# The left tap of a three-tap convolution, moved from VectorE to a ScalarE copy and a GpSimd add

## The reference, cut to what matters

```
def conv_ffn(h, w_up, conv_w, conv_b, w_down):     # h: 256 tokens x 1024
    u = h @ w_up                                    # 256 x 5632
    up = jnp.pad(u, ((0, 0), (1, 1), (0, 0)))
    u = sum(up[:, i:i + S] * conv_w[i] for i in range(3)) + conv_b
    a, b = jnp.split(u, 2, axis=-1)                 # 2816 features each
    return (gelu(a) * b) @ w_down
```

## Time and profile before

| | us |
|---|---|
| median of 3 runs | 2159.01 |
| lowest and highest of them | 2156.7, 2159.69 |
| the profiled execution, whole time | 2157.69 |
| its span, first to last instruction | 2155.9 |
| TensorE busy in it | 2129.4 (99%) |
| VectorE busy | 1491.9 (69%) |
| ScalarE busy | 989.4 (46%) |
| GpSimd busy | 376.3 (17%) |

### The profile page before, as it was taken

One profiled execution on the slowest core, in us unless ns is written; L12 is line 12 of the kernel. 1 busy time (PEld: TensorE's weight loads), 2 busy tenths in 40 slices (PEclk: granted clock), 3 DMA queues, 4 the chain that ended last, 5 costly groups with the idle time before them and its releaser, 6 DMA issues.

```text
span 2155.9 us, 36935 instructions
## 1 busy us (share of the span) xinstructions
PE 2129.4 (99%) x14280; PEld 1939.2 (90%) x14280; DVE 1491.9 (69%) x2157; ACT 989.4 (46%) x1462; POOL 376.3 (17%) x262
## 2 busy tenths in 40 slices
PE   8999999999999999999999999999999999999998
PEld 8999999999999999999877788888888788899998
DVE  7756988876656899968987524798433375866554
ACT  3544456544444555645245433342242244755453
POOL 0410303300500212303301012120020021121120
PEclk9999999999999999999999999999999999999999
DMA  8766667786575556672554323266532244664552
GB/s 316 285 225 204 234 221 249 243 279 211 196 234 176 199 203 207 213 237 90 184 179 153 98 88 105 94 201 215 193 108 98 78 137 153 209 215 157 186 186 98
DMA packets 109450, 396.56 MB, mean 184 GB/s; under 512 B 12264, under 2 KB 12912, under 8 KB 108912
## 3 DMA queue, kind: packets, MB, share of 16 engines
q1 hardware_dynamic: 108016, 390.18, 53.7%
q0 software_dynamic: 1280, 4.20, 0.6%
HBM read 393.28 MB, written 1.05 MB: 183 GB/s over the span
## 4 chain that ended last, share of the span: by engine, by line
PE 90%; DVE 7%; ACT 1%; DMA 1%; issue 1%; SPq 0%; POOL 0%; DVEq 0%; ACTq 0%; POOLq 0%
PE bank L475 24%; PE bank L476 23%; PE bank L477 23%; PE bank L601 3%; DVE w_lo L1337 2%; PE bank L530 2%; PE bank L529 2%; PE bank L528 2%; PE bank L660 1%; DVE stage L1358 1%; PE bank L560 1%; PE bank L571 1%; PE bank L823 1%; DMA stage<-in_stream 1%; PE bank L870 1%
## 5 line engine op out<-in xcount | busy, mean ns | idle before, releaser
L1337 DVE TENSOR_TENSOR w_lo<-stage,w_hi 128x1024 fp32r<-128x1024 f32 x536 | 691.7, 1303 | 508.2 <-ACT w_hi L945 507.8
L945 ACT ACTIVATE w_hi<-stage 128x1024 fp32r<-128x1024 f32 x536 | 566.6, 1060 | 880.9 <-PE bank L477 651.1
L475 PE MATMUL bank<-h_hi,w_hi 128*128 128x256 f32 (+1 forms) x2592 | 800.6, 309 | 6.3 <-DVE w_lo L1337 4.6
L476 PE MATMUL bank<-h_lo,w_hi 128*128 128x256 f32 (+1 forms) x2592 | 794.7, 307 | 0.0
L477 PE MATMUL bank<-h_hi,w_lo 128*128 128x256 f32 (+1 forms) x2592 | 794.5, 307 | 0.0
L475 PEld LDWEIGHTS bank<-h_hi,w_hi 128*128 128x128 f32 x2592 | 494.9, 191 | 37.4 <-DVE w_lo L1337 7.6
L476 PEld LDWEIGHTS bank<-h_lo,w_hi 128*128 128x128 f32 x2592 | 495.0, 191 | 23.2 <-issue 0.7
L477 PEld LDWEIGHTS bank<-h_hi,w_lo 128*128 128x128 f32 x2592 | 494.9, 191 | 22.6
L1358 DVE SCALAR_TENSOR_TENSOR stage<-stage,cvec 128x1024 f32<-128x1024 f32 x192 | 258.9, 1349 | 12.6 <-DMA stage<-in_stream 8.9
L475 PE MATMUL bank<-f_hi,w_hi 128*128 128x512 f32 (+1 forms) x512 | 173.6, 339 | 0.0
L476 PE MATMUL bank<-f_lo,w_hi 128*128 128x512 f32 (+1 forms) x512 | 173.2, 338 | 0.0
(11 more groups left out here) (223 smaller groups left out, 3055.2 us busy)
## 6 DMA issues: line engine op xcount, KB each, us to landing
stage<-in_stream SPq DMA_DIRECT2D x728, 512.0 KB, 4.3
bias<-in_bias POOLq DMA_DIRECT2D x16, 256.0 KB, 3.2
X<-in_x SPq DMA_DIRECT2D x2, 1024.0 KB, 7.0
cvec<-in_cvec SPq DMA_DIRECT2D x3, 512.0 KB, 4.1
decay<-in_decay SPq DMA_DIRECT2D x1, 1024.0 KB, 7.7
out<-X SPq DMA_DIRECT2D x4, 256.0 KB, 2.1
rope<-in_rope SPq DMA_DIRECT2D x2, 256.0 KB, 5.5
dfts<-in_dfts SPq DMA_DIRECT2D x1, 512.0 KB, 6.8
```

The costliest lines, as they stand in the source:

```text
L475: mm(out, w_hi[:, slot, w], xh[:, c, 0:T], start=first, stop=False)
L476: mm(out, w_hi[:, slot, w], xl[:, c, 0:T], start=False, stop=False)
L945: A(w_hi[:, m % NR, :], stage[:, n % NS, :], ACT.Copy).then_inc(hi_ready, 1)
L1337: do(V.tensor_tensor(w_lo[:, m % NR, :], stage[:, n % NS, :], w_hi[:, m % NR, :].bitcast(F32), ALU.subtract), unit_done, n + 1)
```

## The change: what it does

A tile `tap` is added (8 KB a partition, in scratch space whose other users are not live in these blocks). For each bank ScalarE now issues two operations: the middle tap as before, and `tap` = bank times the left weight, a scaled copy; `lin_ready` is counted with the second. VectorE's four left taps go, and with them the wait for their completion ahead of the right taps; the right taps stay, each behind its `lin_ready`. GpSimd waits until all four banks are taken, and adds `tap`, shifted by one token, to `conv` for all four groups in one operation of 4 x 255 elements a partition. Gelu waits for that add (`tap_added`) instead of for the right tap.

```diff
@@ ScalarE
                 def gelu(b):
-                    wait_taken(act, grp(L, f"up{b}", 1))
+                    act.wait_ge(s["tap_added"], L * (FC // 2) + b + 1)
                     A(conv[:, b % 2, 0:2, :], conv[:, b % 2, 0:2, :], ACT.Gelu).then_inc(s["gelu_ready"], 1)
...
                         A(conv[:, b % 2, n, :], bank_of(g)[:, 0:S], ACT.Identity,
-                          bias=col(f"convb_{L}", ch), scale=col(f"convw_{L}", 2 * FC + ch)).then_inc(s["lin_ready"], 1)
+                          bias=col(f"convb_{L}", ch), scale=col(f"convw_{L}", 2 * FC + ch))
+                        A(tap[:, b % 2, n, :], bank_of(g)[:, 0:S], ACT.Copy,
+                          scale=col(f"convw_{L}", ch)).then_inc(s["lin_ready"], 1)
@@ VectorE
                     for n in range(4):
                         ch = 2 * b + n if n < 2 else FC + 2 * b + n - 2
-                        u = bank_of(g0 + n)
                         dve.wait_ge(s["lin_ready"], 4 * it + n + 1)
-                        do(V.scalar_tensor_tensor(y[:, n, 1:S], u[:, 0:S - 1], col(f"convw_{L}", ch), y[:, n, 1:S],
-                                                  ALU.mult, ALU.add))
-                    settle()
-                    for n in range(4):
-                        ch = 2 * b + n if n < 2 else FC + 2 * b + n - 2
                         take(V.scalar_tensor_tensor(y[:, n, 0:S - 1], bank_of(g0 + n)[:, 1:S], col(f"convw_{L}", 4 * FC + ch),
                                                     y[:, n, 0:S - 1], ALU.mult, ALU.add), g0 + n)
@@ GpSimd
                     y = conv[:, b % 2, :, :]
+                    for n in range(4):
+                        wait_taken(pool, grp(L, f"up{b}", n))
+                    G.tensor_tensor(y[:, :, 1:S], y[:, :, 1:S], tap[:, b % 2, :, 0:S - 1], ALU.add).then_inc(s["tap_added"], 1)
                     pool.wait_ge(s["gelu_ready"], it + 1)
-                    wait_taken(pool, grp(L, f"up{b}", 3))
                     G.tensor_tensor(y[:, 2:4, :], y[:, 0:2, :], y[:, 2:4, :], ALU.mult).then_inc(s["u_ready"], 1)
```

More of the change, by code:

```diff
@@ L239, in program @@
         conv = sb("conv", [P, 2, 4, S], F32, tmp)
+        tap = sb("tap", [P, 2, 4, S], F32, tmp + 8 * KB)
         relu = sb("relu", [P, 4, T2], F32, tmp)
@@ L310, in program @@
             "t_ready", "hhi_ready", "h_ready", "xf_ready", "uq_rot", "uk_rot", "fhi_ready", "g_sig", "sq2_ready",
-            "rstd2_ready", "yn_ready", "rhi_ready", "r_ready", "m_ready", "mhi_ready", "mm_ready", "lin_ready",
+            "rstd2_ready", "yn_ready", "rhi_ready", "r_ready", "m_ready", "mhi_ready", "mm_ready", "lin_ready", "tap_added",
             "gelu_ready", "u_ready", "uhi_ready", "uu_ready", "pooled_ready", "phi_ready", "vvar_ready",
```

## The result

| | median us | lowest and highest | runs |
|---|---|---|---|
| before | 2159.35 | 2156.7, 2159.71 | 4 |
| after | 2174.78 | 2173.98, 2177.15 | 4 |

A forecast was written before the change was run, and what follows sets the result against it. TensorE was taken to bind, with VectorE just behind it. 2157.69 us plus 3 in layer 0 and 2.2 in layer 1 gave 2162.9 profiled, and 1.3 more for the median, 2164.2; range 2160.5 to 2170, wide 2157.5 to 2173.

The forecast's parts named there:

- What bounds the kernel, and what can be won: Whole kernel: TensorE binds, VectorE just behind; directly winnable is only TensorE's 1.4 us wait for a w_lo in layer 1.
- The copies: ScalarE in each block: new copy 0.37 us start to start, four pairs 3.3 us instead of 1.9; copies of 0.47 us.
- An add costs VectorE 2.2 us when it meets it: VectorE's w_lo or modulation behind the taps: loses 2 x 1.10 us to GpSimd's add, against 1.7 us saved a block.
- The sum without the chain: Layers 0 and 1: TensorE's longer waits for VectorE, 3 and 2.2 us, nothing for a gelu kept waiting by the add.
- The two terms: Layer 0: 3 us, bounds 0 and 5.3; layer 1: 2.2 us, bounds -1.4 and 5.
- The add's own duration: GpSimd's add in each of 22 blocks: 2.36 us, taken from a row of the same form.
- the neutral one: Rival: the add falls into VectorE's free time, TensorE doesn't wait in layer 0; 2157.6 or 2159 us, chance 0.30.
- upper bound: GpSimd's add: 3.37 us at most, from the average of a row of 1024 elements.
- The gelu holds ScalarE up: Rival, layers 0 and 1: late add delays gelu and next w_hi, some 1 us each late block; around 2174, chance 0.17.
- w_lo that is late issues a refill late, which has units in hand: Weight DMAs: a late w_lo only delays a refill that has units in hand; no cost entered in the sum.
- The range: Total time: own range 2160.5 to 2170 us; wide one, with the neutral rival and part of the chain, 2157.5 to 2173.
- The signs named: Profile after: stretched w_lo, TensorE's waits some 5 to 8 us; gelu waiting for GpSimd in most blocks would mean slower.

The follow-up runs named there:

- e1: The changed kernel without GpSimd's add, the gelu waiting for VectorE's right taps, the left tap missing from the result: 2155.88 us, ratio 0.9989 to before.
- e4: The changed kernel without GpSimd's add and without ScalarE's tap copies, the left tap left out altogether: 2156.91 us, ratio 0.9992 to before.
- e7: The whole changed kernel with ScalarE's gelu one w_hi later and u_hi behind the four pairs: 2165.59 us, ratio 1.0033 to before.
- e2: The changed kernel with the full-length add working on tap alone, the gelu waiting only for the right taps: 2165.49 us, ratio 1.0031 to before.
- e5: The kernel before, complete, with ScalarE's four copies to tap added to each block, read by nobody: 2161.67 us, ratio 1.0017 to before.
- e12: The changed kernel, add in two halves, the first beside the taps of banks 2 and 3, gelu waiting for both: 2159.81 us, ratio 1.0007 to before.

## Why the prediction was wrong, step by step

- **What bounds the kernel, and what can be won:** right. TensorE binds; e1 and e4 won 1.9 and 0.9 us where 1.4 was the most; the difference is within the noise.
- **The copies:** right. 486 ns where 0.47 us was expected, and four pairs take 3.4 us in layer 0 (3.3). The right taps kept their 472 ns.
- **An add costs VectorE 2.2 us when it meets it:** right. The `w_lo` of 373.20 lost 3.37 - 1.22 = 2.15 us. From 300 to 440 us VectorE's busy time is 132.61 in after and 110.67 in e1, 21.9 us or 2.2 an add for the 10 that begin there.
- **The sum without the chain, 5.2 us more than before:** near the 6.7 and 7.7 us of e7 and e2, which have no chain or little of it, but in part by luck. TensorE's waits for `w_lo` in the two stretches are 7.2 us in e7 and 6.7 in e2, within the 5 to 8 expected. The two terms are mis-sized in opposite directions. For layer 0, 3 us were forecast and e7 waits 0.3, e2 1.6. For layer 1, 2.2 us more than before's 1.4 were forecast; e7 waits 6.9 (785 to 998 us), 5.5 more, and e2 5.1, 3.7 more.
- **The add's own duration, and with it the sum's leaving out of the gelu's wait:** this step failed. "I take 2.36, since that one has the new add's form" is what an add takes that begins when issued. The forecast priced the add as VectorE's loss alone. That "GpSimd waits for VectorE as well" it had read off the product's 3.21 us, but used in the rivals only: as relief in the neutral one, as one `w_lo` in front of the add in the gelu's. In the place where the change puts the add, directly ahead of back-to-back operations of VectorE, it waits for 0.8, 1.96 or 3.09 us first, and the "upper bound" of 3.37 us was passed by 8 of 22. The gelu's wait that came of it, 26.0 us in 16 blocks, cost 8 to 9 us, and the sum had nothing for it.
- **"The gelu holds ScalarE up", 0.17, around 2174:** this is what happened, at 2174.78. Its price of 8 to 13 us in all holds at the low end: 8.7 us between after and e7. But the gelu waited in 16 blocks, so that is some 0.5 us a block and not 1, and the good fit of the total is in part luck. The grounds for its low chance failed. Its condition, taps that end under 3.4 us before the gelu, was met in the third block: they ended at 345.19, since a pair of `w_lo` had taken 5.42 us from 333.69, and the gelu could run at 348.14. An add of 2.39 us would still have fitted in, one of 4.35 did not. The argument against it, "TensorE's waits give time back to all of the chain", fell too: from 300 to 380 us TensorE waited 0.5 us for `w_lo`, while ScalarE's slack in that stretch went from 24.4 us to 6.8.
- **"w_lo that is late issues a refill late, which has units in hand":** wrong in layer 0. ScalarE's waits for the weights' DMA went from 6.5 us to 16.2, one of 3.54 at 372.11. By themselves waits of that kind cost little: e5 has 12.1 us of them there and e7 12.5, with TensorE's waits for `w_lo` 0 and 0.3 us. What they add to the gelu's wait, no run separates.
- **The range:** its end of 2173 lay below the time of this rival itself, which it should have held.
- **The signs named:** the last sentence of the prediction named this outcome, waits of the gelu in most blocks with `w_hi` late behind it, and it is what the profile shows.

What stays open: by what rule GpSimd gets in between two operations of VectorE, and whether the copies, which take 11.8 us of ScalarE's slack in layer 0, make the chain dearer: no run has the add on the gelu's path without them.

## What to carry to other kernels

In this kernel, an operation moved to GpSimd with operands in SBUF had two prices, what VectorE loses beside it and what it waits itself when VectorE runs without a gap. The second went to everyone who waited for the result, so price the moved operation at the longest duration of its neighbours, not at the shortest, if something stands behind it in another engine's queue. Put such operations beside VectorE's work on PSUM: cut in two, with the first half there, the same add left a loss of 2 us instead of 15, and cut in two without it, of 19.5. And ask first what the relieved engine is worth: here 37 us of VectorE's work bought 1 to 2 us.

## What the runs showed of the hardware

- GpSimd's add of 1020 float32 elements a partition takes 2.39 us when VectorE is idle at its start (5 of 22), and about 3.2, 4.35 or 5.48 us when issued into back-to-back VectorE operations with two SBUF inputs: it waits for the one under way and up to two more. A half of 510 takes 1.29 us when VectorE is idle or reads PSUM beside it (e12).
- At an accumulator read of VectorE's (0.08 us) it got in, eight times of eight in layer 0: each of these adds ended 2.3 us behind the start of the read.
- VectorE adds the same 1020 elements in 1.22 us.
